# Sparse attention: the step pipeline begun behind the last query chunk, the last four projection chunks laid between and into its steps, one bank pair for the scores

## The chip, the cores and the metric

One of the cores of a Trainium2 chip runs the whole program; seven cores stand idle. The metric is the device time of one execution in microseconds (us). The engines are called TensorE (PE in the profile; PEld are its weight loads), VectorE (DVE), ScalarE (ACT), GpSimd (POOL) and SyncE (SP), which only issues transfers.

## The reference, cut to what matters

The program is two transformer stacks behind one another; the change touches the mixer of the second stack, which runs in each of its two layers (512 tokens, model width 1024). Cut to that mixer:

```
z = h @ w_in                      # q, kc, vc, ks, vs, kw, vw, gates, bg, cg, xc
# attention: 8 heads in 2 key groups, head width 64, queries in 4 blocks of 128
o_cmp = softmax(q . kc' , blocks already past) . vc'    # kc', vc': compressed blocks of 32 tokens, every 16
o_slc = softmax(rope(q) . rope(ks), causal) . vs        # 8 blocks of 64, of which up to 16 are chosen: all
o_win = softmax(rope(q) . rope(kw), causal, 512) . vw
attn  = g0 * o_cmp + g1 * o_slc + g2 * o_win            # g = sigmoid(gates)
# convolution group
conv  = bg * causal_conv3(cg * xc)
out   = concat(rms_norm(attn), rms_norm(conv)) @ w_out
```

## The kernel before, in words

All dense products run in split precision: weights and activations are each held as a rounded part and a remainder, and a product takes three matmuls (lo x hi, hi x lo, hi x hi). Weights come in **chunks** of 256 output columns (1 MB each). A ring of four buffers holds them: SP loads a chunk when the one four places before is finished (L2352), ACT rounds it (`split_next`, L637 to 645), POOL subtracts to get the remainder in four instructions (L2384), and TensorE does 48 matmuls of 128x512 with it (`chunk_products`, L413). ACT's list of splits is written out by hand and stands two chunks ahead of TensorE. DVE takes each result out of PSUM (`take`, L2085), which frees its bank pair. PSUM has four bank pairs: `main0` and `main1` for chunks in turn (`group_slot`, L463), `misc0` and `misc1` for everything else.

The mixer (`nsa_tensor` L1690, `nsa_scalar` L1931, `nsa_vector` L2084) has 16 projection chunks. Chunk 12 holds the second half of the queries, chunks 13 and 14 the second halves of cg and xc, chunks 15 and 16 bg. Chunks 17 to 20 are the output projection. Before the change the order on TensorE is: chunk 12, gates' transposes, chunk 13, the rotation of the second query half (`turn_q(1)`), the compressed scores, chunk 14, transposes of the compressed probabilities, chunk 15, chunk 16 with the scores of steps 0 and 1 in it, and then the rest of the **step pipeline**.

There are 24 steps (`STEPS`, L1655 to 1663). Steps 0 to 7 are query block 3 (512 keys), 8 to 15 block 2 (384 keys); each has one head pair m and one branch (selected or window). Steps 16 to 19 are block 1 (256 keys) and 20 to 23 block 0 (128 keys), each with both branches. Step s goes through the engines like this:

- TensorE `scores(s)` (L1757 to 1772) into a bank pair that alternates (`score_view`, L1678: misc1 for step 0, then main0 and main1). It waits until the maxima of step s-2 have been read.
- DVE adds the mask and takes the row maxima (L2277), one instruction per head and branch.
- ACT does the exponential with the row sum (L2055).
- DVE `shares` (L2240 to 2252): reciprocal of the sums, times the gates, scaling of the probabilities.
- TensorE `turn` (L1774 to 1783): transposes; ACT copies them to SBUF (L2047); TensorE `values` (L1785 to 1796) adds their products with the values in misc1 (bank m[3] for blocks 3 and 1, m[2] for 2 and 0). At a block's start `compressed_values` (L1821) opens the bank; at its end ACT copies it out and squares it (L2037, L2040), and DVE sums the squares (`group_sums`, L2259).

In iteration s of each engine's loop TensorE does scores s, turn s-2, values s-3; DVE the maxima of s, then the shares of s-1.

The **convolution group** shares these engines. DVE: `conv` (L2153 to 2161) and `gated` (L2171) for each half; ACT: squares (L2061); DVE: two sums (L2284, L2285); TensorE: `half_sums` (L1833, the sums over the partitions, recorded at L490); ACT: the square root (L2065), which needs another activation table than the exponential; DVE: reciprocal (L2290); TensorE: `half_spread` (L1837, recorded at L505); DVE: two multiplications (L2295); ACT: four rounded copies to `hid_hi` (L2071); DVE: four remainders (L2302). Before the change, counted in steps: squares in 3, sums in 4, half_sums in 5, root in 6, reciprocal in 7, half_spread in 8, multiplications in 9 and 10, copies in 11 to 14, remainders in 12 to 15.

Behind the steps TensorE goes on with the output projection (recorded at L1901), which begins with the convolution half of its rows.

## Time and profile before

| what | value |
|---|---|
| median of 3 runs | 3218.84 us (3215.92 to 3219.0) |
| profiled execution | 3219.82 us |
| its span, first to last instruction | 3217.7 us |
| mean granted TensorE clock | 0.997 |
| TensorE busy | 3171.8 us (99%) |
| VectorE / ScalarE / GpSimd busy | 1168.1 (36%) / 1185.8 (37%) / 1463.5 us (45%) |
| one weight split on ScalarE (L642) | 1910 ns, 275 of them |
| one remainder on GpSimd (L2384) | 1350 ns, four to a chunk |
| one chunk's load (1 MB) | 4.8 us from issue to landing |
| steps, scores 2 to output projection | layer 0: 1693.34 to 1765.89, layer 1: 2714.78 to 2788.98 |

A busy share is the time in which an engine has at least one instruction under way. Matmuls overlap one another, so a row's duration is longer than the distance to the next; where a price per matmul is wanted, the distance between two starts is read. Idle time of an engine that nobody waits for costs nothing.

### The profile page before, as it was taken

To read this page: it belongs to the slowest core of one execution; us is meant where nothing else is said; L and a number is where in the kernel's file an instruction comes from. 1 tells how busy PE (TensorE), PEld (TensorE's weight loads), DVE (VectorE), ACT (ScalarE), POOL (GpSimd) and SP (SyncE) were. 2 spreads that over 40 slices of the span, in tenths; PEclk is the share of its full clock that TensorE was granted. 3 is DMA by queue.
4 is the path that set the end of the run, shared out by engine and by line. 5 is a ranking of instruction groups with operands and counts; after the bars stand their busy time and mean duration, and the time that the engine had idled before them with its cause. 6 is when DMAs were issued, how large, how long until landed. Compare 5 with 4: busy or idle time off the path is not lost.

```text
span 3217.7 us, 39225 instructions
## 1 busy us (share of the span) xinstructions
PE 3171.8 (99%) x15716; PEld 2602.9 (81%) x15716; DVE 1168.1 (36%) x1727; ACT 1185.8 (37%) x1432; POOL 1463.5 (45%) x1116
## 2 busy tenths in 40 slices
PE   9999999999999999999999999999999999999998
PEld 7888888888888888888776888888888877788887
DVE  6534331343434112211858522104221376742212
ACT  4544332434443233322428423224322243742322
POOL 4335544433554554444650454454444382154443
PEclk9999999999999999999999999999999999999999
DMA  4113223212222222222420222222222241022222
GB/s 163 66 54 117 91 96 113 97 66 90 94 91 104 99 98 104 91 105 105 141 82 15 79 96 99 98 100 90 104 91 105 83 163 69 21 86 101 95 102 94
DMA packets 47672, 302.53 MB, mean 94 GB/s; under 512 B 5680, under 2 KB 8752, under 8 KB 12352
## 3 DMA queue, kind: packets, MB, share of 16 engines
q1 hardware_dynamic: 42480, 292.85, 25.5%
q10 hardware_dynamic: 5072, 7.90, 0.8%
q8 instruction: 97, 1.59, 0.2%
q14 instruction: 23, 0.19, 0.0%
HBM read 296.54 MB, written 2.10 MB: 93 GB/s over the span
## 4 chain that ended last, share of the span: by engine, by line
issue 46%; POOL 35%; PE 16%; ACT 1%; DVE 1%; DMA 0%; POOLq 0%; SPq 0%; ACTq 0%; DVEq 0%
POOL w_lo L2384 35%; PE main L430 13%; PE main L1901 1%; PE main L572 1%; ACT b_p L2055 0%; DMA stage<-in_w 0%; DVE b_p L2277 0%; ACT b_pT L2047 0%; PE misc L490 0%; DVE b_p L2252 0%; DVE y L892 0%; POOLq L98 0%; POOLq L2382 0%; PE main L1770 0%; PE misc L1792 0%
## 5 line engine op out<-in xcount | busy, mean ns | idle before, releaser
L2384 POOL TENSOR_TENSOR w_lo<-stage,w_hi 128x512 fp32r<-128x512 f32 x1100 | 1448.7, 1350 | 1722.7 <-ACT w_hi L642 1722.7
L430 PE MATMUL main<-h_hi,w_lo 128*128 128x512 f32 x2456 | 961.4, 391 | 1.1 <-POOL w_lo L2384 0.7
L430 PE MATMUL main<-h_lo,w_hi 128*128 128x512 f32 x2456 | 956.6, 390 | 0.0
L430 PE MATMUL main<-h_hi,w_hi 128*128 128x512 f32 x2456 | 956.5, 389 | 0.0
L642 ACT ACTIVATE w_hi<-stage 128x2048 fp32r<-128x2048 f32 x275 | 523.0, 1910 | 418.1 <-DMA stage<-in_w 417.0
L430 PEld LDWEIGHTS main<-h_hi,w_lo 128*128 128x128 f32 x2456 | 461.7, 188 | 103.0 <-issue 7.2
L430 PEld LDWEIGHTS main<-h_hi,w_hi 128*128 128x128 f32 x2456 | 461.5, 188 | 96.6
L430 PEld LDWEIGHTS main<-h_lo,w_hi 128*128 128x128 f32 x2456 | 461.7, 188 | 94.9 <-issue 0.5
L430 PE MATMUL main<-hid_hi,w_lo 128*128 128x512 f32 x1168 | 454.5, 389 | 0.0
L430 PE MATMUL main<-hid_hi,w_hi 128*128 128x512 f32 x1168 | 454.4, 389 | 0.0
L430 PE MATMUL main<-hid_lo,w_hi 128*128 128x512 f32 x1168 | 454.4, 389 | 0.0
L430 PEld LDWEIGHTS main<-hid_hi,w_lo 128*128 128x128 f32 x1168 | 219.2, 188 | 45.7 <-issue 0.2
L430 PEld LDWEIGHTS main<-hid_hi,w_hi 128*128 128x128 f32 x1168 | 219.2, 188 | 45.6
L430 PEld LDWEIGHTS main<-hid_lo,w_hi 128*128 128x128 f32 x1168 | 219.2, 188 | 45.4
L826 DVE TENSOR_TENSOR val<-main,rstd 128x1024 f32<-128x1024 f32 x60 | 73.5, 1224 | 461.1 <-PE main L430 461.1
L695 ACT ACTIVATE hid_hi<-val 128x1024 f32 (+1 forms) x66 | 69.9, 1059 | 371.2 <-DVE val L832 371.2
L806 DVE TENSOR_TENSOR gate<-main,rstd 128x1024 f32<-128x1024 f32 x66 | 80.8, 1224 | 328.3 <-PE main L430 299.2
L859 DVE TENSOR_SCALAR y<-main,par 128x512 f32<-128x512 f32 x48 | 36.0, 750 | 378.3 <-PE main L430 330.3
L836 DVE TENSOR_TENSOR hid_lo<-val,hid_hi 128x1024 f32 (+1 forms) x66 | 89.4, 1355 | 93.0 <-ACT hid_hi L695 93.0
L690 ACT ACTIVATE sq<-gate 128x1024 f32<-128x1024 f32 x44 | 46.7, 1061 | 184.6 <-DVE gate L824 184.1
L851 DVE TENSOR_TENSOR x<-main,x 128x1024 f32<-128x1024 f32 x16 | 19.6, 1225 | 246.0 <-PE main L430 246.0
L832 DVE TENSOR_TENSOR val<-val,sq 128x1024 f32<-128x1024 f32 x66 | 86.3, 1307 | 7.8
(342 smaller groups left out, 3145.2 us busy)
## 6 DMA issues: line engine op xcount, KB each, us to landing
stage<-in_w SPq DMA_DIRECT2D x275, 1024.0 KB, 4.8
x<-in_xT SPq DMA_DIRECT2D x8, 256.0 KB, 5.1
out_x<-x ACTq DMA_DIRECT2D x4, 512.0 KB, 2.6
stage<-in_w SPq DMA_DIRECT2D x8, 128.0 KB, 6.1
stage<-in_w SPq DMA_DIRECT2D x2, 512.0 KB, 7.4
b_r<-sq ACTq DMA_DIRECT2D x4, 256.0 KB, 7.1
b_r<-sq ACTq DMA_DIRECT2D x4, 255.5 KB, 8.6
ev_ws<-in_ev_ws ACTq DMA_DIRECT2D x1, 512.0 KB, 6.0
```

The costliest lines, as they stand in the source:

```text
L430: last = pe.matmul(acc[:, m, :], w[a], r[b], start=start and k == 0 and j == 0, stop=stop and k == nk - 1 and j == 2)
L572: last = pe.matmul(acc[:, m, :], w[a], r[b], start=start and k == 0 and j == 0, stop=k == nk - 1 and j == 2)
L642: act.activation(c.w_hi[:, s, :, :].rearrange("p k n -> p (k n)"), c.stage[:, s, :], ACT.Copy)\
L690: e.activation(c.sq[:, :, :], c.gate[:, :, 2:], ACT.Silu).then_inc(c.act_ready, 1)
L695: e.activation(two(c.hid_hi, i), c.val[:, :, :], ACT.Copy).then_inc(c.hid_hi_done, 1)
L806: e.tensor_tensor(c.gate[:, :, 2:], c.ps[n.slot()][:, :, :], rstd, ALU.mult)\
L826: e.tensor_tensor(c.val[:, :, :], (c.mp[1] if extra else c.ps[n.slot()])[:, :, :], rstd, ALU.mult)\
L832: e.tensor_tensor(c.val[:, :, :], c.val[:, :, :], c.sq[:, :, :], ALU.mult)\
L836: e.tensor_tensor(two(c.hid_lo, i), c.val[:, :, :], two(c.hid_hi, i).bitcast(F32), ALU.subtract).then_inc(c.hid_lo_done, 1)
L859: return dve.tensor_scalar(c.y[:, 2 * m + b, :], acc[:, b, :], c.par[:, col:col + 1], None, ALU.mult)
L1901: last = pe.matmul(acc[:, m, :], w[a], r[b], start=start and k == k0 and j == 0, stop=stop and k == k0 + 3 and j == 2)
L2384: last = e.tensor_tensor(c.w_lo[:, s, k:k + 2, :].rearrange("p k n -> p (k n)"), c.stage[:, s, k * CW:(k + 2) * CW], c.w_hi[:, s, k:k + 2, ...
```

## The change

- TensorE: the gates' transposes move into chunk 12 (before its sixth k tile). Chunk 13 is done in three pieces by the new function `chunk_tiles`: k tiles 0 and 1; then the query rotation, the compressed scores and scores 0; k tiles 2 to 4; scores 1; k tiles 5 to 7. Chunks 14, 15 and 16 are done in three pieces each inside steps 2 to 10 (`FILL`), between turn and values, all in the same bank pair (`same_slot`). The compressed probabilities' transposes stand in step 2, before turn 0.
- All scores go to one bank pair, the other one than the chunks'. Scores s waits for the maxima of step s-1, and scores 0 for the rotated queries.
- The convolution group: the takes stand in steps 2, 5, 8 and 11, the second half's convolution in steps 5 and 6, the gatings in 8 and 11. The rest of its chain is counted from `CONV_STEP` = 11: squares in 12, sums in 13, half_sums in 14, root in 15, reciprocal in 16, half_spread in 17, both multiplications in 18, copies in 20 to 23, remainders in 21 to 24. Its sums use bank m[3] instead of m[2], so that `compressed_values(1)` (step 19) waits for the multiplications instead of `compressed_values(2)` (step 11). Its squares go to other tiles.
- ACT: the mask's transfer is issued behind the rotated queries, two weight splits stand in steps 4 and 8, the copies of the compressed probabilities in step 2.
- DVE: the product with the cosine stands before the wait for the rotation; the normalizing of the compressed probabilities stands behind the maxima of step 0.

```diff
+def chunk_tiles(pe, n, c, acc, k0, k1):
+    s = n.chunk % RING
+    if k0 == 0:
+        pe.wait_ge(c.w_lo_done, n(c.w_lo_done))
+    for k in range(k0, k1):
+        for m in range(2):
...
+            for j, (a, b) in enumerate(((1, 0), (0, 1), (0, 0))):
+                last = pe.matmul(acc[:, m, :], w[a], r[b], start=k == 0 and j == 0, stop=k == KT - 1 and j == 2)
+    if k1 == KT:
+        last.then_inc(c.chunk_done, 1)
+        n.chunk += 1
+def same_slot(pe, n, c):
+    pe.wait_ge(c.group_taken, n.group)
+    n.skip(c.group_taken)
+    n.group += 1
+    n.flip += 1
+    return c.ps[n.slot(-1)]
+FILL = {2 + 3 * j + q: r for j in range(3) for q, r in enumerate(((0, 3), (3, 6), (6, KT)))}
+CONV_STEP = 11
 def score_view(c, l, s):
-    return c.mp[1] if s == 0 else c.ps[(s - 1 + c.score_slot[l]) % 2]
+    return c.ps[c.score_slot[l]]
@@ scores
-        if s < 3:
-            pe.wait_ge(c.group_taken, n.group - (s < 2))
+        if s == 0:
+            pe.wait_ge(c.q_roped, 2 * l + 2)
         else:
-            pe.wait_ge(c.a_max, 64 * l + exps_until(s - 1))
+            pe.wait_ge(c.a_max, 64 * l + exps_until(s))
@@ compressed_values, half_sums
-        if i == 2:
+        if i == 1:
             pe.wait_ge(c.half_done, n(c.half_done, 2))
-        pe.wait_ge(c.a_sum, 5 * l + 1)
-        token_sums(pe, c.m[2], c.ones, c.acc[:, 0, :], True, True).then_inc(c.half_ssq, 1)
+        pe.wait_ge(c.a_sum, 5 * l + 2)
+        pe.wait_ge(c.a_oT, 4 * l + 1)
+        token_sums(pe, c.m[3], c.ones, c.acc[:, 0, :], True, True).then_inc(c.half_ssq, 1)
@@ TensorE's order
-    z()
-    rope_was_read()
-    gates_turn()
-    z()
+    z(at={5: lambda: (rope_was_read(), gates_turn())})
+    acc = group_slot(pe, n, c)
+    c.score_slot[l] = n.slot()
+    chunk_tiles(pe, n, c, acc, 0, 2)
     pe.wait_ge(c.a_gate_exp, l + 1)
     turn_q(1)
     pe.wait_ge(c.tok_copied, n(c.tok_copied))
     compressed_scores()
-    z()
-    rope_was_read()
-    compressed_prob_turn()
-    z()
-    c.score_slot[l] = n.slot(1)
-    z(at={4: lambda: scores(0), 6: lambda: scores(1)})
+    scores(0)
+    chunk_tiles(pe, n, c, acc, 2, 5)
+    scores(1)
+    chunk_tiles(pe, n, c, acc, 5, KT)
     for s in range(2, N_STEPS + 3):
         if s < N_STEPS:
             scores(s)
-        if s == 5:
+        if s == 2:
+            rope_was_read()
+            compressed_prob_turn()
+        if s == CONV_STEP + 3:
             half_sums()
-        if s == 8:
+        if s == CONV_STEP + 6:
             half_spread()
         if 2 <= s < N_STEPS + 2:
             turn(s - 2)
+        if s in FILL:
+            if FILL[s][0] == 0:
+                acc = same_slot(pe, n, c)
+            chunk_tiles(pe, n, c, acc, *FILL[s])
@@ ACT's steps
+        if s == 2:
+            for hh in range(2):
+                act.wait_ge(c.a_probT, 50 * l + hh + 1)
+                act.activation(c.b_pcT[:, hh, :], c.m[hh][:, :], ACT.Copy).then_inc(c.a_copied, 1)
-        if s == 3:
+        if s in (4, 8):
+            split_next(act, n, c)
+        if s == CONV_STEP + 1:
             act.wait_ge(c.conv_done, n(c.conv_done))
...
-        if s == 6:
+        if s == CONV_STEP + 4:
             act.wait_ge(c.half_ssq, n(c.half_ssq))
...
-        if 11 <= s < 15:
+        if CONV_STEP + 9 <= s < CONV_STEP + 13:
@@ DVE's steps
         if s == 2:
-            take(c.val[:, :, :])
-            gated(1)
-            signal(c.conv_done)
+            take(c.b_u[1][:, :, :])
+        if s in (5, 8, CONV_STEP):
+            take_again(c.val[:, :, :])
...
+        if s == 0:
+            compressed_shares()
         if 1 <= s <= N_STEPS:
             shares(s - 1)
-        if s == 4:
+        if s == 5:
+            conv_input(1)
+            conv_taps(2)
+        if s == 6:
+            conv_taps(3)
+        if s == 8:
+            gated(0)
+        if s == CONV_STEP:
+            gated(1)
+            signal(c.conv_done)
+        if s == CONV_STEP + 2:
...
-        if s == 7:
+        if s == CONV_STEP + 5:
...
-        if 9 <= s < 11:
-            if s == 9:
-                dve.wait_ge(c.half_spread, n(c.half_spread))
-            x = c.b_y[:, 2 * s - 18:2 * s - 16, :]
-            dve.tensor_tensor(x, x, over_tiles(c.m[2][:, :]), ALU.mult).then_inc(c.half_done, 1)
+        if s == CONV_STEP + 7:
+            dve.wait_ge(c.half_spread, n(c.half_spread))
+            for j in range(2):
+                x = c.b_y[:, 2 * j:2 * j + 2, :]
+                dve.tensor_tensor(x, x, over_tiles(c.m[3][:, :]), ALU.mult).then_inc(c.half_done, 1)
-        if 12 <= s < 16:
+        if CONV_STEP + 10 <= s < CONV_STEP + 14:
```

## Rows read from the trace of the kernel before

**Rows 1.** Waits of TensorE in the steps of layer 0: total, times, longest (us).
```profile
PE misc L1781 <- DVE b_p L2252: 2.4, 4, 1.1
```
**Rows 2.** Stretches of layer 0: length, busy us per engine, clock, DMA share, GB/s.
```profile
1693.30:1723.60 30.30, 28.46 (x262) 19.23 (x262) 24.10 (x76) 25.04 (x56) 0.00 (x0) 1.00 0.08 34
...
1723.60:1765.90 42.30, 39.54 (x417) 28.61 (x415) 37.52 (x167) 39.68 (x130) 0.00 (x0) 1.00 0.01 2
...
1742.80:1765.20 22.40, 21.16 (x243) 16.26 (x241) 19.56 (x106) 22.35 (x80) 0.00 (x0) 1.00 0.01 2
```
**Rows 3.** Timeline of TensorE where scores 0 interrupts chunk 16: start, duration, what.
```profile
1683.59 0.39 PE L430 MATMUL main<-h_hi,w_hi 128*128 128x512 f32 x1
1683.91 1.13 PE L1770 MATMUL misc<-b_k,b_qr 64*128 64x512 f32 x4
1684.97 0.50 PE L430 MATMUL main<-h_hi,w_lo 128*128 128x512 f32 x1
1685.31 0.39 PE L430 MATMUL main<-h_lo,w_hi 128*128 128x512 f32 x1
1685.54 0.40 PE L430 MATMUL main<-h_hi,w_hi 128*128 128x512 f32 x1
```
**Rows 4.** Timeline of TensorE in the steps of layer 0; idle time in brackets.
```profile
1693.34 1.13 PE L1770 MATMUL main<-b_k,b_qr 64*128 64x512 f32 x4 [1.31 <-DVE val L2087]
...
1705.37 1.05 PE L490 MATMUL misc<-ones,acc 128*128 128x1 f32 x8 [1.36 <-DVE acc L2285]
1706.29 1.07 PE L1781 MATMUL misc<-ident,b_p 128*128 128x128 f32 x8
...
1708.31 1.13 PE L1770 MATMUL main<-b_k,b_qr 64*128 64x512 f32 x4
...
1711.42 1.13 PE L1770 MATMUL main<-b_k,b_qr 64*128 64x512 f32 x4
...
1715.38 0.65 PE L505 MATMUL misc<-ident,col 128*128 128x128 f32 x4
...
1729.74 0.92 PE L1770 MATMUL main<-b_k,b_qr 64*128 64x384 f32 x4
...
1732.20 0.92 PE L1770 MATMUL main<-b_k,b_qr 64*128 64x384 f32 x4
```
**Rows 5.** Timeline of ACT in the steps of layer 0.
```profile
1700.88 1.05 ACT L2061 ACTIVATE val<-b_y 128x1024 f32<-128x1024 f32 x1
...
1712.57 1.28 ACT L2065 ACT_TABLE_LOAD   x1
1713.87 0.26 ACT L2065 ACTIVATE col<-misc,stat 128x4 f32<-128x4 f32 x1
...
1715.12 1.28 ACT L2055 ACT_TABLE_LOAD   x1
...
1736.46 0.71 ACT L2071 ACTIVATE hid_hi<-b_y,par 128x512 fp32r<-128x512 f32 x1
```
**Rows 6.** Timeline of DVE in layer 0: a product beside GpSimd and without, sums, scaling.
```profile
1626.36 2.20 DVE L2155 TENSOR_TENSOR b_u<-b_u,val 128x1024 f32<-128x1024 f32 x1
...
1668.05 1.23 DVE L2155 TENSOR_TENSOR b_u<-b_u,val 128x1024 f32<-128x1024 f32 x1
...
1703.37 1.22 DVE L2284 TENSOR_TENSOR sq<-sq,val 128x1024 f32<-128x1024 f32 x1
1704.63 0.69 DVE L2285 TENSOR_TENSOR acc<-sq 128x512 f32<-128x512 f32 x1
...
1721.19 1.22 DVE L2295 TENSOR_TENSOR b_y<-b_y,misc 128x1024 f32<-128x1024 f32 x1
```
**Rows 7.** Layer 1 behind the wait for the sums: a stretch, then TensorE's timeline.
```profile
2728.00:2730.00 2.00, 2.00 (x20) 1.83 (x20) 1.10 (x4) 1.60 (x4) 0.00 (x0) 0.69 0.00 0
...
2728.73 1.97 PE L1792 MATMUL misc<-b_pT,b_va 128*64 128x128 f32 x16
2730.63 1.89 PE L1770 MATMUL main<-b_k,b_qr 64*128 64x512 f32 x4
```

More of the change, by code:

```diff
@@ L2020, in nsa_scalar @@
     split_next(act, n, c)
+    act.wait_ge(c.q_roped, 2 * l + 2)
+    act.dma_start(c.b_amask[:, :], a["b_amask"]).then_inc(c.b_masks_loaded, 16)
     act.wait_ge(c.a_cmp_sub, l + 1)
-    act.dma_start(c.b_amask[:, :], a["b_amask"]).then_inc(c.b_masks_loaded, 16)
     act.activation(c.b_p[:, 2, :, :], c.b_p[:, 2, :, :], ACT.Exp).then_inc(c.a_cmp_exp, 1)
-    split_next(act, n, c)
-    for hh in range(2):
-        act.wait_ge(c.a_probT, 50 * l + hh + 1)
-        act.activation(c.b_pcT[:, hh, :], c.m[hh][:, :], ACT.Copy).then_inc(c.a_copied, 1)
-    split_next(act, n, c)
     groups = 0
@@ L2151, in flat, with conv_input, conv_taps @@
             n.skip(c.a_lo_done)
[L2153 removed]
+    def conv_input(j):
         u = c.b_u[j]
         step(dve.tensor_tensor(u[:, :, :], u[:, :, :], c.val[:, :, :], ALU.mult))
[L2156 to L2161 removed]
+    def conv_taps(m):
+        u = c.b_u[m // 2]
+        w = [c.par[:, PC["cw"] + 12 * l + 4 * k + m:][:, 0:1] for k in range(3)]
+        step(dve.tensor_scalar(c.b_y[:, m, :], u[:, m % 2, :], w[2], None, ALU.mult))
+        for k, s in ((1, 1), (0, 2)):
+            step(dve.scalar_tensor_tensor(c.b_y[:, m, s:], u[:, m % 2, 0:T - s], w[k],
+                                          c.b_y[:, m, s:], ALU.mult, ALU.add))
     def hidden(kv):
@@ L2209, in nsa_vector @@
     rope_k(1)
-    conv(0)
+    conv_input(0)
+    conv_taps(0)
+    conv_taps(1)
     take(c.b_q[:, 2:4, :], HD ** -0.5)
@@ L2227, in nsa_vector, with compressed_shares, take_again @@
         .then_inc(c.a_cmp_sub, 1)
-    dve.wait_ge(c.a_cmp_exp, l + 1)
-    step(dve.tensor_reduce(cst, prob, AX.X, ALU.add))
-    step(dve.reciprocal(cst, cst))
-    rows = c.b_cst[:, :, :].rearrange("p h (i m) -> p h i m", i=TT)
-    step(dve.tensor_tensor(rows, rows, c.b_g[:, :, 0:8].rearrange("p i (h m) -> p h i m", h=2), ALU.mult))
-    dve.tensor_tensor(prob, prob, cst.unsqueeze(2).to_broadcast([P, 32, 32]), ALU.mult)\
-        .then_inc(c.a_cmp_norm, 1)
-    take(c.val[:, :, :])
-    conv(1)
-    take(c.val[:, :, :])
-    gated(0)
+    def compressed_shares():
+        dve.wait_ge(c.a_cmp_exp, l + 1)
+        step(dve.tensor_reduce(cst, prob, AX.X, ALU.add))
+        step(dve.reciprocal(cst, cst))
+        rows = c.b_cst[:, :, :].rearrange("p h (i m) -> p h i m", i=TT)
+        step(dve.tensor_tensor(rows, rows, c.b_g[:, :, 0:8].rearrange("p i (h m) -> p h i m", h=2), ALU.mult))
+        dve.tensor_tensor(prob, prob, cst.unsqueeze(2).to_broadcast([P, 32, 32]), ALU.mult)\
+            .then_inc(c.a_cmp_norm, 1)
+    def take_again(dst):
+        n.flip += 1
+        take(dst)
     def shares(s):
```

41 lines of the change are left out of this document (18 added, 23 removed).

## Prediction

> **What bounds the kernel now.** TensorE is nearly always busy over the whole run, and the change touches only the sparse-attention stage, which runs once in each of two layers. So only TensorE time inside that stage can be won. I read three views of it: the waits, the stretches and the timelines. The stage has two kinds of TensorE work: projection chunks (48 matmuls, one every 0.23 us [rows 3]) and 24 attention steps. In a step TensorE does scores, eight transposes ("turn") and value products; DVE takes the row maxima and scales the probabilities; ACT does the exponentials and copies the turned probabilities out of PSUM.
>
> In the waits of layer 0, TensorE stands still for DVE's scaled probabilities four times, 2.4 us together [rows 1]. The timeline adds 1.31 us before scores 2 and 1.36 us before the conv group's sum of squares [rows 4]. Those are the holes that chunk work could fill, some 5 us and in the other layer the same.
>
> The stretches show what lies beneath. From scores 2 to scores 11 (30.3 us) ACT is busy for 25.0 and DVE for 24.1, so both have room. From scores 11 to the output projection (42.3 us) ACT is busy 39.7, DVE 37.5, TensorE 39.5. In the last 22.4 us of that, ACT is busy for 22.35: there ACT, not TensorE, sets the pace [rows 2]. I call the first stretch the front and the second the tail. The question is what each gets.
>
> **The front.** The three chunks that stood ahead of the steps now lie in steps 2 to 10, nine pieces of 12 to 18 matmuls, 2.7 to 4.1 us each, and a fourth is split around scores 0 and 1. A full-width step of 3.1 us (scores 7 behind scores 6 [rows 4]) becomes one of 6 to 7.4 us, against some 2.5 us of ACT and DVE work in a step. So the waits in the front go: 1.4 (scores 2) + 0.3 (the first of the four) + 1.4 (the sum of squares) = 3.1 us. The conv group's sums and spread leave the front too: 0.9 us (the sums start at 1705.37, the next group 0.92 later) and 0.5 us for the spread [rows 4]. They come back in the tail.
>
> What is added: each extra change between chunk matmuls and other ones costs 0.09 us going out (0.32 instead of 0.23) and 0.11 coming back (0.34 instead of 0.23) [rows 3]. There were five such pairs, there will be twelve: 7 x 0.2 = 1.4 us. The compressed probabilities' transposes now stand directly before turn 0, which must wait until ACT has emptied the same banks: a copy of half a microsecond against half a microsecond of transposes, 0.3 us. Front: -3.1 - 1.4 + 1.7 = **-2.8 us**.
>
> Edits that I cost at nothing, each with its cover. Scores 0 now waits for the rotated queries: TensorE has 12 chunk matmuls, the rotation and the 64 small matmuls of the compressed scores to do while DVE takes, rotates and adds; by my walk the cover is about 1 us, and what DVE is later than that is paid whole. The score mask's DMA is issued on ACT's queue only then and has to land before the first maximum; DVE's maximum and subtraction for the compressed scores cover it, and the 18 chunk matmuls behind scores 0 cover both for TensorE. Two weight splits (1.9 us of ACT each) move from before the steps to steps 4 and 8, where ACT has 4 us to spare; GpSimd's four subtractions behind each of them come later, but their chunks are used only after the steps. SP's loads hang on finished chunks and come later by the same time. One bank pair for scores means that scores s+1 waits for the maxima of step s instead of s-1. In the front a 6 us step covers that. In the tail TensorE has turn and values (1.6 us for 384 keys, 2.0 for 512) against maxima of 1.0 to 1.4 us: covered while DVE is on time, a wait when it is late.
>
> **The tail.** Here comes the bill. The conv group's tail (second gating, squares, sums, square root, spread, scaling, splitting) moves from steps 2 to 15 to steps 11 to 24, so these land in a stretch where ACT and DVE are full:
> - ACT: the two squares, 1.9 us, and the square root with its table load and the exponential's reload, 2 x 1.28 + 0.3 = 2.8 us [rows 5]. The four copies to hid_hi, 0.6 us each start to start, were in steps 11 to 14; they now fall in steps 20 to 23, inside the 22.4 us in which ACT has no gap.
> - DVE: a take and a gating (2.4 us), the sums (1.22 + 0.69) and the scaling, of which one piece of 1.22 was still in the front [rows 6]: 5.5 us.
> ACT's work in the tail becomes 39.7 + 1.9 + 2.8 = 44.4 us, DVE's 37.5 + 5.5 = 43.0 us, both more than the 42.3 us that the tail takes now. That alone is the lower bound: with no idle time at all, 44.4 us, +2.1. The upper bound is the same work with the idle time ACT has now (42.3 - 39.7 = 2.6) and the new waits on top. Of these there are two. The sum of squares: a step is 2.46 us here (1729.74 to 1732.20) instead of 3.11, so its chain of ACT squares and DVE sums has 0.65 us less cover: a wait of about 2.0 instead of 1.36 us [rows 4]. And group 1's first products in step 19 now wait for the conv scaling that DVE does in one piece of 2.3 us in step 18, behind maxima and scaling: about 1.5 us for TensorE, but ACT is busy all the same by then. Taking 44.4 + 2.6 + 1.0 (the waits, as far as ACT starves for them) = **48.0 us**, +5.7 us, is near the upper bound. I take it because walking the three engines' lists step by step leaves ACT idle for some 4 us in steps 12 to 15, where the copy of turn 12 hangs on the sum of squares, and without a gap afterwards.
>
> On table loads the rows show 1.28 us each, with the next activation 0.02 us behind the first [rows 5]. The Trainium skill ("ScalarE: Activation LUTs", What ACT_TABLE_LOAD costs) gives the same 1283 ns and another 1380 ns of drain for every switch. By that page the two switches would be 5.3 us, and the sum 2 x 2.7 us higher; the rows leave no room for such a drain, and I go by them.
>
> Per layer -2.8 + 5.7 = +2.9 us, for both layers **+5.8 us**. The profiled execution took 3219.82 us, 2.1 more than its span of 3217.7, and is 1.0 above the median of the runs, 3218.84; I put the difference on the median: **3224.6 us**, +0.18%. Differences under 0.2% (6.4 us) are about what a measurement of this kernel can't tell from no change.
>
> **The rivals.**
> *A, ACT keeps up (chance 0.22).* The new waits hide in one another and ACT never starves: the tail is 44.4 us. -2.8 + 2.1 = -0.7 per layer, 3217.4 us. For it: ACT's work is packed to within 0.05 us over 22.4 us there already. Against: in the rest of the tail ACT stands for 2.6 us even now.
> *B, the full gain (0.13).* The tail stays at 42.3 us or sheds its own waits too, since more time between chunk and step lets ACT and DVE enter it early. -2.8 x 2 gives 3213.2, and with the clock's fall in layer 1 (below) gone 3211.6. Against it stands the sum of 44.4 us of ACT work.
> *C, the clock falls (0.18, slower).* The granted clock stands at 2.4 GHz nearly throughout. In layer 1, right behind the 1.36 us wait for the sums, it fell to 1.2 GHz (0.69, the mean of a stretch that holds both levels); a step's value products took 1.97 us and the next scores 1.89 where scores take 1.13 [rows 4, 7]; with 0.8 us lost on each, 1.65 us. In layer 0 the same wait cost no fall. With 2.0 us at the sums and 1.5 us in step 19 it may fall at both places in both layers: four falls for one, 3 x 1.65 = 5.0 us, 3229.6 us. It decides if TensorE's idle share at these places exceeds that of 1.36 us in a step. The Trainium skill ("TensorE: Matmul & The Clock Gate", What's actually happening) has it that the throttled rate is the default and activity releases it; the trace agrees, and by that rule the fills protect the front while the tail is more exposed.
> *D, a drain at the table loads (0.03, slower).* Were each load followed by a stop as long as itself, ACT would lose 2 x 1.28 us more per layer: 3229.7 us.
> *E, DVE against GpSimd (0.04, slower).* DVE's product of two SBUF tensors took 2.20 us beside GpSimd's subtractions and 1.23 us without [rows 6]. Step 5 has a take, maxima, shares, the conv input and three taps, 7 us, 10 so slowed, against 7.4 us of TensorE; one step of slack absorbs it. If it did not, 3 us per layer: 3230.6 us.
> That nothing is hidden at all (the chunks only displace, no wait goes) would be +3.1 per layer on top of the forecast and needs front waits that I see no cause for.
>
> **How the numbers follow.** The forecast has 0.40, its own range 3221 to 3228. Outside it, A and B reach down to 3212, C, D and E up to 3231; 3212.5 to 3231 leaves about 2 in 10 out. Faster by over 0.2% (below 3212.4) needs B with some more, and part of my doubt in the tail's walk: 0.14. Slower by over 0.2% (above 3225.3): C, D, E and somewhat under half of the forecast: 0.42. Within: 0.44.
>
> **What would show it.** In the changed kernel: scores 11 comes about 2.8 us earlier after chunk 12's start; steps 2 to 10 show no idle time on TensorE over 0.3 us; the wait for the sums of squares is near 2 us and stands in step 14; the first group-1 products wait for the conv scaling; ACT is busy over 97% from step 15 to the last value product, and scores 11 to output projection takes about 48 us. If that stretch is under 44 us, or TensorE's waits there sum to less than 5 us, the forecast's mechanism is wrong; if TensorE waits inside steps 2 to 10, the front is.

## The result, and the profile after

The changed kernel took **3235.99 us** (median of 5 runs, 3230.44 to 3238.7) against 3218.84 us before, ratio 1.0053 [1.0042, 1.0063]: 17 us slower, where +5.8 was forecast and 3231 was the top of the range. The profiled execution took 3234.93 us, its span is 3232.8 us.

Three views are needed, in this order. First TensorE's waits in the changed kernel (total, times, longest, us):

```profile
PE misc L1809 <- DVE b_p L2293: 6.2, 6, 1.4
...
PE misc L516 <- DVE acc L2339: 4.0, 2, 2.0
...
PE misc L1858 <- DVE b_y L2349: 3.1, 2, 1.5
PE misc L1820 <- ACT b_pT L2081: 1.7, 2, 0.9
```

The wait for the sums of squares is 2.0 us, the one for the scaling 1.5: both as forecast. Both layers are in these rows: scaled probabilities are now waited for 3.1 us in a layer, 2.4 before [rows 1]. Next the stretches of the changed kernel: chunk 12 to scores 11 (the front) and scores 11 to the output projection (the tail), first layer 0, then layer 1 (length; busy us of PE, PEld, DVE, ACT, POOL; clock; DMA share; GB/s):

```profile
1627.36:1723.14 95.78, 95.44 (x583) 69.81 (x581) 62.10 (x120) 36.17 (x72) 27.42 (x20) 0.96 0.16 56
1723.14:1774.20 51.06, 43.23 (x428) 31.50 (x426) 41.55 (x171) 43.68 (x131) 0.00 (x0) 0.95 0.07 22
...
2659.11:2751.79 92.68, 92.34 (x583) 68.07 (x582) 62.04 (x120) 36.17 (x72) 27.40 (x20) 1.00 0.16 58
2751.79:2803.76 51.97, 44.10 (x428) 32.02 (x426) 41.54 (x171) 43.68 (x131) 0.00 (x0) 0.93 0.06 21
```

The same cuts in the kernel before, beside the tail shown in [rows 2]:

```profile
1625.57:1723.63 98.06, 94.94 (x595) 71.56 (x594) 64.18 (x124) 39.95 (x74) 28.15 (x20) 0.98 0.18 65
...
2648.59:2746.70 98.11, 94.99 (x595) 71.29 (x592) 64.34 (x124) 39.95 (x74) 28.17 (x20) 0.98 0.18 65
2746.70:2788.98 42.28, 39.52 (x417) 28.59 (x415) 37.51 (x166) 39.66 (x130) 0.00 (x0) 1.00 0.01 2
```

The front became 2.3 and 5.4 us shorter, the tail 8.8 and 9.7 us longer. The two layers differ in the clock column, which stands at 1.00 in one front and at 0.96 in the other. The third view is therefore TensorE's timeline in step 14, in the changed kernel's layer 0:

```profile
1734.59 1.18 PE L516 MATMUL misc<-ones,acc 128*128 128x1 f32 x8 [2.00 <-DVE acc L2339]
1735.63 1.52 PE L1809 MATMUL misc<-ident,b_p 128*128 128x128 f32 x6
1737.08 1.55 PE L1820 MATMUL misc<-b_pT,b_va 128*64 128x128 f32 x12
```

and in layer 0 of a second profile of the same kernel (run e11 below), where the clock stayed up:

```profile
1728.98 1.05 PE L516 MATMUL misc<-ones,acc 128*128 128x1 f32 x8 [2.00 <-DVE acc L2339]
1729.89 0.85 PE L1809 MATMUL misc<-ident,b_p 128*128 128x128 f32 x6
1730.68 0.88 PE L1820 MATMUL misc<-b_pT,b_va 128*64 128x128 f32 x12
```

The same transposes take 1.52 us instead of 0.85 and the same value products 1.55 instead of 0.88: 1.2 GHz instead of 2.4 (a stretch of 3 us there, 1735 to 1738, has a granted clock of 0.56). Where no fall stands behind step 14, the changed kernel's stage looks like this (e11, layer 0; the fourth row is where the low clock does stand in that layer, from 1.1 us before the tail's end on):

```profile
1624.88:1717.52 92.64, 92.30 (x583) 68.08 (x582) 62.01 (x120) 36.19 (x72) 27.52 (x20) 1.00 0.17 58
1717.52:1767.04 49.52, 41.66 (x429) 30.26 (x427) 41.55 (x171) 43.60 (x131) 0.00 (x0) 0.99 0.06 23
...
1735.00:1765.90 30.90, 25.36 (x278) 19.23 (x276) 27.27 (x125) 30.39 (x97) 0.00 (x0) 1.00 0.01 1
1765.90:1769.40 3.50, 3.41 (x14) 2.60 (x15) 1.04 (x1) 1.13 (x3) 0.00 (x0) 0.51 0.00 0
```

Step 23 with what follows it takes 9.89 us in this layer and 9.43 in layer 1 of the first profile, where no fall stands at the tail's end. So a tail of 49.5 us holds 0.45 us of lower clock, and without any fall the changed kernel's tail is 49.07 us.

So the loss has two parts, and every run gives an estimate of them: its time multiplied by its mean granted clock is about what it would take at 2.4 GHz throughout, the rest counts as lost to the lower clock. (The clock is listed to three digits, 1.6 us on one run either way, so I use means.) Over the 72 runs of the kernel before in all comparisons that is 3209.3 us and 8.9 us lost; over 10 runs of the changed kernel 3215.5 and 19.7. By this estimate **+6.2 us are the order of the work and +10.8 us are the clock.**

The estimate counts too much as lost, in both kernels. In the kernel before the clock is low in the last 7.7 us, where TensorE has no matmul:

```profile
3210.00:3217.70 7.70, 0.00 (x0) 0.00 (x0) 4.43 (x4) 0.00 (x0) 0.00 (x0) 0.50 0.63 253
```

And in e6 below it was low between the two layers' stages:

```profile
2599.00:2606.00 7.00, 6.02 (x29) 6.05 (x30) 6.93 (x6) 1.38 (x1) 5.54 (x4) 0.51 0.14 57
```

Yet from layer 0's output projection to layer 1's chunk 12 e6 takes 882.60 us, and the kernel before, with half as much time at the low clock there, 882.69.

The stretches give a second estimate. Without a fall the front goes from 96.35 to 92.66 us and the tail from 42.27 to 49.07: +3.1 us a layer. And 1.0 us a layer lies outside front and tail. 20 us before chunk 12 TensorE waits for GpSimd's remainder of a chunk's weights, 0.37 us in the kernel before and 1.34 in the changed one. Before, layer 1 (TensorE, the subtraction that it waits for, DVE's product with the cosine):

```profile
2629.09 0.47 PE L430 MATMUL main<-h_hi,w_lo 128*128 128x512 f32 x1 [0.37 <-POOL w_lo L2384]
2627.69 1.25 POOL L2384 TENSOR_TENSOR w_lo<-stage,w_hi 128x512 fp32r<-128x512 f32 x1
2629.57 1.71 DVE L2125 TENSOR_TENSOR gate<-b_q,b_cos 128x1024 f32<-128x1024 f32 x1
```

and after:

```profile
2639.60 0.47 PE L431 MATMUL main<-h_hi,w_lo 128*128 128x512 f32 x1 [1.34 <-POOL w_lo L2438]
2637.20 2.25 POOL L2438 TENSOR_TENSOR w_lo<-stage,w_hi 128x512 fp32r<-128x512 f32 x1
2636.64 1.68 DVE L2158 TENSOR_TENSOR gate<-b_q,b_cos 128x1024 f32<-128x1024 f32 x1
```

The change moved this product ahead of DVE's wait for the rotation. It now runs beside the subtraction, which takes 2.25 us instead of 1.25, and TensorE waits for it. The wait is 1.33 to 1.37 us in 28 of the 30 layers of the kernels with this edit, the hybrid e9 among them, which takes back the moves of ACT's splits and of DVE's takes; it is 0.37 us at most in the kernel before, e1 and e6, which do not have it. And e12, whose layer 0 has no fall at its tail's end either, takes 883.54 us from there to layer 1's chunk 12, 0.9 more than the kernel before. No run takes this edit back alone. Together that is 4.1 us a layer: by the stretches some 8 of the 17 us are the order of the work and some 9 the clock.

### The profile page after: what moved, and what is told of

Same layout as the page of the kernel before. It is cut to its first block, busy times and chain, and to the rows that moved or that the text cites. A ratio compares the mean times of both kernels' runs of the same rounds, so it can differ in the third digit from the quotient of the medians.

```text
span 3232.8 us, 39223 instructions
## 1 busy us (share of the span) xinstructions
PE 3177.9 (98%) x15716; PEld 2603.7 (81%) x15716; DVE 1171.2 (36%) x1727; ACT 1185.8 (37%) x1432; POOL 1463.5 (45%) x1116
## 4 chain that ended last, share of the span: by engine, by line
issue 46%; POOL 35%; PE 16%; ACT 1%; DVE 1%; DMA 0%; POOLq 0%; SPq 0%; ACTq 0%; DVEq 0%
POOL w_lo L2438 35%; PE main L431 11%; PE main L447 1%; PE main L1935 1%; PE main L598 1%; PE main L1798 1%; DMA stage<-in_w 0%; PE misc L1809 0%; PE misc L1820 0%; ACT b_p L2089 0%; PE misc L516 0%; DVE b_p L2318 0%; DVE y L918 0%; POOLq L98 0%; POOLq L2436 0%
## 5 line engine op out<-in xcount | busy, mean ns | idle before, releaser
L431 PE MATMUL main<-h_hi,w_lo 128*128 128x512 f32 x2328 | 910.5, 391 | 3.5 <-POOL w_lo L2438 3.2
L431 PE MATMUL main<-h_lo,w_hi 128*128 128x512 f32 x2328 | 906.3, 389 | 0.0
L431 PE MATMUL main<-h_hi,w_hi 128*128 128x512 f32 x2328 | 906.2, 389 | 0.0
L431 PEld LDWEIGHTS main<-h_hi,w_lo 128*128 128x128 f32 x2328 | 437.3, 188 | 97.9 <-issue 7.0
L431 PEld LDWEIGHTS main<-h_hi,w_hi 128*128 128x128 f32 x2328 | 437.3, 188 | 90.9
L431 PEld LDWEIGHTS main<-h_lo,w_hi 128*128 128x128 f32 x2328 | 437.4, 188 | 90.1 <-issue 0.5
L845 DVE SCALAR_TENSOR_TENSOR sq<-gate,par,sq 128x512 f32<-128x512 f32 x88 | 72.3, 842 | 45.8 <-ACT sq L709 39.7
```

The lines of the kernel that those rows point to most:

```text
L431: last = pe.matmul(acc[:, m, :], w[a], r[b], start=start and k == 0 and j == 0, stop=stop and k == nk - 1 and j == 2)
L845: e.scalar_tensor_tensor(c.sq[:, j, :], c.gate[:, j, k:k + T], c.par[:, bass.ds(col + 2 * i + j, 1)], c.sq[:, j, :], ALU.mult, ALU.add).th ...
```

## The experiments

All ratios are to the kernel before on the same chip. "At full clock" is the product just named, "lost" the rest. Front and tail are us in one profiled layer; those with * hold a fall of the clock that lengthens them by over 1 us. The tails of 49.4 and 49.5 without a * and e7's 51.6 hold 0.45 us of a fall at their end.

| run | median us (runs) | ratio | at full clock / lost | front | tail |
|---|---|---|---|---|---|
| before | 3217.8 (72) | 1 | 3209.3 / 8.9 | 98.1* | 42.3 |
| e11, changed kernel again | 3233.39 (5) | 1.0057 [1.0043, 1.0071] | 3215.2 / 20.1 | 92.6 | 49.5 |
| e1, conv late alone | 3233.39 (4) | 1.005 [1.0033, 1.0067] | 3213.8 / 18.6 | 93.5 | 49.4 |
| e2, two pairs from step 12 | 3233.72 (4) | 1.0047 [1.003, 1.0063] | 3217.3 / 15.4 | 92.7 | 49.5 |
| e3, waits filled, too much | 3234.25 (4) | 1.005 [1.0033, 1.0067] | 3217.5 / 17.0 | 92.6 | 51.2 |
| e3b, waits filled, less | 3230.58 (5) | 1.0038 [1.0024, 1.0052] | 3217.2 / 12.9 | 92.7 | 49.5 |
| e4, conv three steps earlier | 3230.45 (5) | 1.0037 [1.0023, 1.0052] | 3215.6 / 14.2 | 94.1* | 50.6* |
| e5, dense fills, conv early | 3221.97 (11) | 1.0011 [1.0002, 1.002] | 3211.7 / 10.3 | 95.6* | 45.2 |
| e10, the same, two pairs | 3221.0 (10) | 1.0008 [0.9999, 1.0018] | 3210.7 / 10.3 | 95.6* | 45.1 |
| e6, before, sums a step later | 3215.47 (10) | 0.9993 [0.9983, 1.0002] | 3208.1 / 8.0 | 95.0 | 43.1 |
| e9, hybrid | 3214.78 (11) | 0.9991 [0.9982, 1.0] | 3206.0 / 9.4 | 95.3* | 43.0 |
| e7, ACT dose, steps 20 to 23 | 3235.8 (4) | 1.0054 [1.0038, 1.0069] | 3218.6 / 17.0 | 92.7 | 51.6 |
| e12, DVE dose, steps 20 to 23 | 3228.44 (5) | 1.0037 [1.0022, 1.0051] | 3215.8 / 13.6 | 92.7 | 49.1 |
| e13, ACT dose, steps 13, 14 | 3231.52 (4) | 1.0046 [1.003, 1.0063] | 3215.6 / 17.0 | 92.7 | 49.5 |
| e15, DVE dose, steps 12 to 14 | 3234.67 (4) | 1.0052 [1.0035, 1.0069] | 3214.4 / 20.2 | 92.7 | 52.4* |
| e8, no table loads | 3232.99 (4) | 1.0047 [1.0032, 1.0062] | 3212.0 / 20.2 | 92.7 | 49.4* |
| e14, changed, sums a step later | 3233.8 (4) | 1.0045 [1.0028, 1.0061] | 3216.4 / 17.8 | 92.7 | 49.4 |

### Which part of the change costs

**e1: the kernel before, with nothing but the conv group's tail moved.**

```
-  if s == 5: half_sums()            (squares 3, root 6, spread 8, scaling 9 and 10)
+  if s == 14: half_sums()           (squares 12, root 15, spread 17, scaling 18)
```

> The kernel before, with the convolution group's chain alone moved to where the change has it (squares in step 12 to remainders in 21 to 24, sums in bank m[3], group 1 waiting for the scaling); chunks, scores' banks and everything else as before. Theory T (the loss is the chain in the full tail): the stretch from scores 11 to the output projection grows from 42.3 us to 49 to 52 us in both layers, the front loses its 1.4 us wait and 1.4 us of work, total +10 to +14 us over before. Rival R (the loss comes from the single score bank pair, or from the fills): within 3 us of before.

3233.39 us, 15 over the kernel before where 10 to 14 were expected: nearly the whole loss without a single chunk moved. Its stretches and its waits:

```profile
1624.28:1717.79 93.51, 91.89 (x584) 69.09 (x582) 61.66 (x122) 35.55 (x69) 28.14 (x20) 1.00 0.19 68
1717.79:1767.15 49.36, 41.50 (x429) 30.28 (x427) 40.41 (x170) 44.17 (x135) 0.00 (x0) 0.99 0.01 1
```

```profile
PE misc L490 <- DVE acc L2289: 4.3, 2, 2.1
...
PE misc L1831 <- DVE b_y L2299: 3.1, 2, 1.5
PE main L1771 <- DVE val L2090: 2.6, 2, 1.3
```

The tail is the changed kernel's. The front lacks the sums, the spread and the 1.36 us wait; against it the nine pieces of chunks gain only 0.85 us more (93.51 to 92.66).

**e2: the changed kernel with both bank pairs for the scores from step 12.**

```
+  return c.ps[(c.score_slot[l] + max(s - 11, 0)) % 2]      # scores(s) waits for the maxima of s - 2
```

> The changed kernel, with the scores alternating between both bank pairs from step 12 on, so that scores s waits for the maxima of step s-2 again. Theory T: the single pair costs only the 0.2 us wait at scores 14, so the time stays within 2 us of the changed kernel (about 3235). Rival R (one bank pair ties TensorE to DVE's lateness in the tail): the tail shrinks by 3 us or more a layer, 3229 us or less.

The tail stays at 49.5 us. The single pair isn't the cause.

**e4: conv group three steps earlier, the fills as halves of chunks in steps 2 to 7.**

```
-  FILL: steps 2 to 10, CONV_STEP = 11
+  FILL: steps 2 to 7, CONV_STEP = 8
```

> The changed kernel with each chunk laid into two steps instead of three (24 matmuls a piece, steps 2 to 7) and the convolution's chain counted from step 8 instead of 11 (takes in 4, 6, 8; splits in 3 and 6). Theory T: squares, sums and root fall into steps 9 to 12, the copies to hid_hi into 17 to 20; from scores 11 on ACT has some 4 us less to do, the sum of the attention stage shrinks by 3 to 5 us a layer, total 3225 to 3229 us. Rival R (fills as such cost, or the bank pair): within 2 us of the changed kernel.

3230.45 us, above the 3225 to 3229 that I expected. Two waits went and two came (TensorE's waits in e4):

```profile
PE main L1798 <- DVE b_nmax L2318: 4.7, 4, 1.6
PE misc L516 <- ACT sq L2070: 4.6, 2, 2.3
```

The sums use bank m[3], and three steps earlier ACT has not emptied it yet.

### Is it TensorE's idle time, or the clock behind it?

**e3 and e3b: matmuls that nothing reads in front of the two waits.**

```
+  for _ in range(k): pe.matmul(<free pair>[:, 0, 0:P], c.ident, c.ones)    # e3: 15 and 11, e3b: 8 and 6
```

> The changed kernel, with 15 small matmuls without use ahead of the wait for the sums of squares (step 14) and 11 ahead of the wait for the scaling (step 19), so that TensorE is active in these waits. Theory C (the falls of the clock behind these waits cost time of their own): no half-rate stretch behind step 14, the tail 1.5 to 3 us shorter a layer, total 3 to 6 us under the changed kernel. Rival (ACT's list sets the tail, what TensorE loses to the clock is hidden in it): the falls go but the time moves by less than 1.5 us.

e3 missed its 3 to 6 us: steps 14 and 19 became 6.7 and 6.4 us long instead of 5.4 and 5.6, a tail of 51.2 us. So a smaller dose was run beside the unchanged kernel.

> The changed kernel with 8 matmuls of 128 columns whose result nothing reads before the wait for the sums of squares, and 6 before the one for the scaling (15 and 11 were too many: they made the two steps longer). TensorE's idle time at both places is then under 0.5 us, the steps as long as without them. If the clock's falls behind these waits are a cause of the loss, no fall stands in steps 14 to 20 and the time is 3 to 6 us under the changed kernel's in the same batch (3229 to 3233 us). Rival: as many windows of low clock turn up elsewhere, so that the time stays within 2 us of it.

> The changed kernel once more, unchanged, in the same batch, as the measure for the others: 3233 to 3238 us, tail 49.4 to 49.5 us wherever the clock does not fall in it.

e3b's tails, layers 0 and 1:

```profile
1719.38:1768.89 49.51, 44.97 (x457) 33.50 (x455) 41.55 (x171) 43.57 (x131) 0.00 (x0) 0.99 0.06 23
...
2746.54:2796.03 49.49, 44.98 (x456) 33.51 (x454) 41.53 (x171) 43.58 (x131) 0.00 (x0) 0.99 0.07 23
```

and e11's tail in layer 1 with what follows it, for the clock:

```profile
2744.60:2797.18 52.58, 45.46 (x429) 32.97 (x427) 41.53 (x171) 43.72 (x131) 0.00 (x0) 0.90 0.06 21
2797.18:2860.00 62.82, 61.90 (x287) 51.91 (x286) 29.83 (x41) 22.84 (x30) 21.85 (x16) 0.95 0.18 68
```

TensorE is busy 45.0 us instead of 41.7, its wait in step 14 is gone and the one in step 19 is 0.2 us, and the stretch is the same to 0.02 us: TensorE's idle time is an effect. But no fall stands behind step 14, where one cost e11's layer 1 3.0 us (scores 20 come 34.85 us after scores 11 there and 31.81 in layer 0). In the nine profiles with a wait of some 2 us for the sums in step 14 and no busy-work (the changed kernel's two, e1, e2, e7, e8, e12, e13, e15), a fall stands behind it in 12 of 18 layers; in e3 and e3b in none of 4. The mean time of the changed kernel's ten runs is 3235.3 us, that of e3b's five 3230.1, 5.2 less, as expected (the medians of e11 and e3b are only 2.8 apart). So the clock is a real part, and one that busy-work takes back only in part: both layers of e3b still have the fall at the tail's end.

### Which engine sets the tail?

**e7, e12, e13, e15: one extra copy of 128 x 512 per step that nothing waits for**, on ACT in steps 20 to 23 (e7) or 13 and 14 (e13), on DVE in steps 20 to 23 (e12) or 12 to 14 (e15).

```
+  act.activation(<unused tile>, c.b_y[:, m, :], ACT.Copy)        # e7, e13
+  dve.tensor_copy(<unused tile>, c.b_y[:, m, :])                 # e12, e15
```

> The changed kernel with one more ACT copy (128 x 512, from b_y into a tile that nothing reads, some 0.6 us) in each of steps 20 to 23, which nothing waits for. If ACT sets the pace from the conv scaling to the output projection, each is paid whole: scores 11 to output projection 2.2 to 2.6 us longer per layer, time 3239.5 to 3242 us. Rival, TensorE or DVE sets it and ACT has slack: nothing per layer, 3235 to 3237 us. In between, the copies are paid in part.

> The changed kernel with one more DVE copy (128 x 512, SBUF to SBUF, nothing reads it) in each of steps 20 to 23, behind which the next maxima stand. If ACT alone sets the pace there, a DVE copy hides: scores 11 to output projection within 0.5 us of 49.5 where the clock does not fall. If DVE sets it too, the dose is paid, 1.2 to 2.4 us per layer. My guess is the first, paid to under a half.

> The changed kernel with one more ACT copy (128 x 512) in each of steps 13 and 14, before the square root, that nothing waits for. By the prediction's walk ACT stands idle there for lack of turn 12's copy, so both hide: tail within 0.4 us of 49.5 where the clock does not fall. Rival: ACT is the bound from the squares on, and the tail grows by the two copies, 1.0 to 1.3 us.

> The changed kernel with one more DVE copy (128 x 512, 0.42 us by the dose in steps 20 to 23, into a tile that is written again before anything reads it) in each of steps 12, 13 and 14. If DVE sets the pace there, all three are paid, scores 11 to output projection is 1.0 to 1.3 us longer where the clock does not fall (50.5 to 50.8). Rival: TensorE's and ACT's own waits set it, the copies hide and the tail stays within 0.4 us of 49.5.

The tails of e7, e12 and e13:

```profile
2752.99:2804.56 51.57, 42.27 (x428) 30.89 (x426) 41.63 (x171) 45.64 (x135) 0.00 (x0) 0.97 0.07 22
```

```profile
2747.62:2796.69 49.07, 41.62 (x428) 29.95 (x426) 42.79 (x175) 43.63 (x131) 0.00 (x0) 1.00 0.06 23
```

```profile
1717.58:1767.09 49.51, 41.64 (x429) 30.26 (x427) 41.54 (x171) 44.51 (x133) 0.00 (x0) 0.99 0.07 23
```

ACT 2.04 us busier late: tail 2.05 us longer, paid whole, all of it behind scores 23, though the median didn't show it (at full clock +3.4 on e11, and 3 us less lost to the clock). DVE 1.24 us busier late: nothing. Its 49.07 us are 0.45 under e11's 49.52 because this layer has no fall at its end (clock column 1.00), which is just what the fall costs there. ACT 0.9 busier early: nothing. e15's layers both hold the fall at step 14. Against e11's layer 1, which holds it too, its layer 1 is 0.4 us longer (52.99), and TensorE reached the sums 0.3 us later: the one copy ahead of DVE's sums was paid, the two behind them were not, where 1.0 to 1.3 us were expected. So DVE sets the pace up to its sums in step 14, ACT from step 16 to the end.

**e8: no table loads.** The square root is replaced by a plain copy; the root of the conv group's mean square is left out of the computation.

```
-  act.activation(c.col[:, 0:4], c.m[3][:, 0:4], ACT.Sqrt, bias=c.eps, scale=1.0 / 512)
+  act.activation(c.col[:, 0:4], c.m[3][:, 0:4], ACT.Copy, scale=1.0 / 512)
```

> The changed kernel with the square root of the conv group's mean square replaced by a plain copy, so that the root is left out and ACT loads no other table in step 15 and none back in step 16: 2.5 us of ACT less in the tail. If ACT sets the tail's pace from there, scores 11 to output projection is 2.0 to 2.6 us shorter per layer, time 3230.5 to 3233 us. Rival: the loads lie where ACT waits anyway (behind the sums, ACT had idle time in steps 12 to 15), tail shorter by under 0.7 us, time within 1.5 us of the changed kernel. If the change were worth over 3 us a layer, a drain at the loads (rival D of the prediction) would be in it.

By the product 3.2 us less than e11, but with four and five runs that is rough, and both its layers hold a fall in steps 14 and 15. The steps behind the fall say it better: step 18 takes 2.89 us against 3.90 and step 19 5.43 against 5.60, the others from 16 on are the same. That is 1.2 us a layer for 2.4 us less of ACT (41.21 against 43.60): paid by half, where 2.0 to 2.6 were expected if ACT set the pace alone.

**e14: the changed kernel with its sums a step later** (`half_sums` in step 15, root 16, reciprocal 17, spread 18).

> The changed kernel with the sums of squares, the root, the reciprocal and the spread one step later each (15, 16, 17, 18); the scaling stays in step 18. If the tail's length is ACT's work plus the idle time that step 14 gives it, the wait of 2.0 us before the sums and ACT's idle time of 2.3 us behind it go, scores 11 to output projection is 1.5 to 2.3 us shorter (47.2 to 48.0 where the clock does not fall), the clock's fall behind step 14 is gone too, and the time is 3226 to 3230 us. Rival: the sums are late by DVE's work and the next hand-over (the scaling, which now waits for a later spread in the same step) takes the same time again: tail 49 us or more, time 3230 us or more.

The rival was right: tail 49.45. Step 14 fell from 5.42 to 3.87 us and step 17 from 3.18 to 2.70, and steps 15 and 19 gave it back (2.46 to 3.35, 5.60 to 6.78). ACT's idle time from scores 11 to step 16 was 4.2 us in e11 and is 4.1 us here, in other places (its timeline, idle time in brackets):

```profile
1722.49 0.87 ACT L2081 ACTIVATE b_pT<-misc 128x384 f32<-128x384 f32 x2 [1.27 <-PE misc L1809]
...
1729.64 0.61 ACT L2089 ACTIVATE b_p<-b_p,b_nmax 128x384 f32<-128x384 f32 x1 [0.49 <-DVE b_nmax L2318]
...
1732.46 0.87 ACT L2081 ACTIVATE b_pT<-misc 128x384 f32<-128x384 f32 x2 [1.51 <-PE misc L1809]
...
1735.14 0.87 ACT L2081 ACTIVATE b_pT<-misc 128x384 f32<-128x384 f32 x2 [0.62 <-PE misc L1809]
```

### Versions with the conv group early

**e6: the kernel before, its sums one step later.**

```
-  sums 5, root 6, reciprocal 7, spread 8
+  sums 6, root 7, reciprocal 8, spread 9
```

> The kernel before with only the sums of squares, the root, the reciprocal and the spread one step later each (6, 7, 8, 9), no chunk moved. My theory of the front is that TensorE's 1.36 us before the sums are a plain wait that one more step covers, and that the clock's fall in layer 1 hangs on it: front 1.3 to 1.4 us shorter per layer, tail 42.3 as before, time 3214 to 3217 us, the fall behind step 5 of layer 1 gone. Rival: ACT and DVE set the steps 3 to 10 too, the idle time turns up at the next probabilities instead: front unchanged within 0.4 us, time 3217 to 3220.

```profile
1626.77:1721.75 94.98, 93.29 (x596) 70.39 (x594) 63.41 (x121) 39.52 (x73) 28.15 (x20) 1.00 0.19 67
1721.75:1764.82 43.07, 39.58 (x417) 28.56 (x415) 38.26 (x172) 40.34 (x131) 0.00 (x0) 1.00 0.01 2
```

The wait for the sums is gone and the clock column is at 1.00: 3.1 us of front in the layer, 0.8 given back in the tail. Only 1.4 of the 3.1 us are the wait. The other 1.7 are layer 0's fall, which stood at 1654 to 1657 in the kernel before, 50 us ahead of this wait, so that its absence here is no work of this edit; layer 1's fall stood behind the wait, and is gone too. In time 2.8 us, at the edge of what these runs can tell: the interval still holds no change.

**e5 and e10: each chunk whole in steps 2, 3 and 4, conv group as early as that allows**, with one pair (e5) or with both from step 15 (e10).

```
+  FILL = {2: (0, KT), 3: (0, KT), 4: (0, KT)}; CONV_STEP = 5      # sums 9, root 10, spread 12, scaling 12 and 13
```

> The changed kernel with the same three chunks laid whole into steps 2, 3 and 4 (one a step, 11 us each) instead of in nine pieces, and the conv group's tail moved back to where it stood: second take in step 5, squares in 6, sums and root in 8 and 9, scaling in two pieces in steps 11 and 12. The sums and the spread are written into the free main bank pair. My theory is that the loss sits in the tail because the conv group's work lands where ACT and DVE are full: then scores 11 to output projection is back at 42 to 43 us, the front stays near 93 us, the waits before the sums and before group 1's first products are gone, and the time is 3209 to 3214 us, faster than both kernels. Rival 1, one bank pair (scores s+1 behind the maxima of s) costs in the tail by itself: tail 45 us or more. Rival 2, any rearrangement is paid back, since ACT then has no lead from the front: front near 96, time 3217 to 3222.

> The dense version (three chunks whole in steps 2 to 4, conv group early) with the scores alternating between both bank pairs from step 15 on. If the single pair is what keeps its tail at 45.2 us (TensorE waited there for maxima, 3.7 us together), the waits for maxima from step 15 on are gone and the tail is 1.5 to 2 us shorter, time 3217 to 3219 us. Rival: DVE is late by itself and each such wait becomes one for the scaled probabilities: tail within 0.5 us of 45.2, time 3220 to 3223.

3221.97 and 3221.0 us: 13 us of the changed kernel's 17 are gone, but e5 misses its 3209 to 3214 us, and both stay above the kernel before. (The sums, the root and the scaling stand a step later in it than the expectation says.) With the scaling at the start of the tail, scores 14 waited 1.7 us for DVE's maxima in both; the second pair turned later waits for maxima into waits for probabilities, as the rival had it.

**e9: a hybrid meant to beat both.** Two more chunks ahead of the steps, one around scores 0 and 1, one in step 2.

```
+  FILL = {2: (0, KT)}; CONV_STEP = 3       # squares 4, sums 7, root 8, spread 10, scaling 10 and 11; two pairs from 13
```

> A version meant to beat both kernels, from what the runs have shown so far: two more chunks stand before the steps again, one is split around scores 0 and 1, and one alone is laid into step 2. The conv group's tail stands one step later than in the kernel before and two steps behind its sum (squares 4, sums 7, root 8, spread 10, scaling in steps 10 and 11), written into the pair that no scores use; from step 13 on the scores alternate between both pairs. By my account the front loses the waits of 1.3 and 0.3 us around scores 2 and the 1.36 us before the sums (front near 93.8 us), the tail is as in the kernel before (42.3 to 43.1), time 3211 to 3215 us. Rival: the waits on DVE only move by a step, as in the dense version: front plus tail at 138 us or more, time 3216 to 3221.

3214.78 us, 0.9991 [0.9982, 1.0] of the kernel before and some 20 us under the changed one: the fastest here, though its lead over e6 is less than these runs can tell. Its front of 95.28 us holds a fall of the clock (0.98), without which it would be near the 93.8 expected; tail 43.0. At full clock it is 3.3 us under the kernel before.

## Why the prediction was wrong

**The direction was right, and so was one of the two places named for the clock; the clock's price was not.** By its own steps:

- *Front, -2.8.* Without a fall of the clock the front before is 96.35 us (e6's 94.98 and the 1.36 it lacks), after 92.66: -3.7. The waits went as said, 0.34 came for the compressed probabilities as said, no other wait stood in steps 2 to 10. The term that was mis-sized is the changes between chunk and other matmuls, 1.4 us. By the timeline of e11 a change costs 0.09 going out and 0.1 back, but the chunk matmul follows the turn after 0.85 us where values follow it after 1.0: net 0.04 a pair, 0.4 us in all.

```profile
1664.80 1.10 PE L1809 MATMUL misc<-ident,b_p 128*128 128x128 f32 x8
1665.65 0.48 PE L447 MATMUL main<-h_hi,w_lo 128*128 128x512 f32 x1
...
1669.94 1.09 PE L1858 MATMUL misc<-b_pcT,b_vbd 128*64 128x128 f32 x16
```

- *Tail, 42.3 to 48.0.* It is 49.5, of which 0.45 are the fall at its end. ACT's work was put at 44.4 and is 43.6; its idle time at 3.6 and is 5.9. The walk had found the 4 us in steps 12 to 15, but the sum added only 1.0 to the 2.6 of before, as if the two overlapped. ACT in e11:

```profile
1722.28 0.87 ACT L2081 ACTIVATE b_pT<-misc 128x384 f32<-128x384 f32 x2 [1.27 <-PE misc L1809]
...
1730.46 0.87 ACT L2081 ACTIVATE b_pT<-misc 128x384 f32<-128x384 f32 x2 [2.28 <-PE misc L1809]
...
1734.99 1.28 ACT L2101 ACT_TABLE_LOAD   x1
1736.28 0.26 ACT L2101 ACTIVATE col<-misc,stat 128x4 f32<-128x4 f32 x1
...
1737.33 1.28 ACT L2089 ACT_TABLE_LOAD   x1
...
1767.16 0.60 ACT L2067 ACTIVATE b_oT<-misc 128x512 f32<-128x512 f32 x1 [1.22 <-PE misc L1820]
```

From 1735.00 to 1765.90 ACT is busy 30.39 of 30.90 us: packed, as forecast. The mistake is to take for a bound one engine's work over the whole stretch where DVE sets the first part and ACT the rest. Net of front and tail without falls +3.1 a layer, 6.2 in all, where 5.8 were forecast. That it comes so close is partly luck: the front's error of -0.9 and the tail's of +1.1 cancel.

- *DVE's product with the cosine, costed nowhere.* It is an edit of the change, but not in the list of those put at nothing. Rival E had the same collision of a DVE product with GpSimd, 2.20 us against 1.23 [rows 6], and looked for it in step 5 alone. Here GpSimd is the one held up, TensorE waits for it, and it costs 1.0 us a layer.

- *The clock, forecast at zero, +10.8 by the product and some 9 by the stretches.* **This is the step that failed.** The working kept the clock's losses as they were and gave rival C, the clock behind the waits of steps 14 and 19, a chance of 0.18 and 5.0 us on the forecast's waits. The mechanism is C's, and step 14 is one of its two places: in e11 the same wait of 2.0 us has a fall behind it in layer 1 and none in layer 0, as its timeline and stretches show. Behind step 19's wait neither profile of the changed kernel has one. The second place is the tail's end: TensorE has idle spots of 0.8, 1.4 and 0.9 us behind scores 23, and the clock fell there in three of the four layers, with the output projection's matmuls to pay for it (e11's layer 0: 0.45 us in the tail; 0.95 is the clock of the stretch behind layer 1). That these spots bring that fall on is argued, not shown: layer 1 of the first profile has the same ones, and no fall. C's price of 1.65 us fits the short fall in layer 0 of the first profile (1735.4 to 1738.8, 1.55 us); the falls behind step 14 in layer 1 of both profiles lasted twice as long (in e11 2755.8 to 2762.7) and cost 2.9 and 3.0. The rule of the Trainium skill ("TensorE: Matmul & The Clock Gate", What's actually happening) that the low clock is the default and activity lifts it is borne out by e3 and e3b, whose busy-work kept the clock up behind step 14. I cited it and gave it too little. I had also not seen that the front before held a fall in layer 0 as well (its clock column says 0.98). That one is behind no wait: it starts 3.8 us after the start of the compressed scores, 64 small matmuls without idle time between them. So do the falls in 16 of the 36 fronts profiled, in the old and the new order (2.7 to 4.7 us after that start), the changed kernel's layer 0 with its 3.1 us among them. Against these the fills protect nothing.
- *Rival A* (ACT keeps up) fell with the 5.9 us of idle time, *B* (the full gain) with the tail. *D*, the drain: the root follows its load after 0.01 us in e11, and leaving both loads out gave 1.2 us a layer, less than the loads' own 2.56. The Trainium skill ("ScalarE: Activation LUTs", What ACT_TABLE_LOAD costs) has a further 1380 ns of drain for each switch; no run here shows it. *E*: steps 2 to 10 had no wait over 0.34 us, so DVE kept up there; its collision came elsewhere, as said.

**Of what the text named as tests:** scores 11 came 3.7 us earlier after chunk 12 (2.8 said, clock left out), steps 2 to 10 had one wait over 0.3 us (0.34, the compressed probabilities', which the sum had), the sums' wait was 2.0 in step 14, group 1's products waited for the scaling, ACT was busy 97% from step 15 to the last value product, the tail was 49.5 (48). Nearly all held, and the time was still wrong, since none of them was a test of the clock.

**What stays open.** Where each unprofiled run lost its time to the clock: the profiled runs show only their own falls, at different places from run to run. What the changed kernel takes with the cosine's product where it was. And why moving the sums in e14 gave nothing at all. That its tail equals the others' to 0.1 us suggests that the hand-overs of the conv group through TensorE, ACT and DVE have to be paid once wherever they stand among full steps, but no run isolates this.

## What to carry to other kernels

Filling TensorE's gaps with foreign matmuls is worth only the gaps. What decides is what has to move to make room: here a chain of eight hand-overs went from steps where DVE and ACT had room [rows 2] into steps where they had none, and one of the two large gaps, with layer 1's fall behind it, was gone from the trace by moving four instructions by one step (e6; the time's interval still holds no change). Bound a stretch by the sum over its parts of whichever engine is full in each, not by one engine's total. Where a change adds idle time of 1 to 2 us to TensorE at several places, price the clock behind each of them as its own term, from traces of several runs; here it was as large as everything else. And give every moved instruction a line in the working, also one that only changes places with a wait: here one nobody priced cost 1.0 us a layer.

## What was not expected of the hardware

The same instructions with the same wait had the lower clock behind them in one layer and not in the other, so that runs of one kernel spread over 9 us (3230.81 to 3239.72) and a dose of 2.05 us a layer didn't show in a median (e7). And a low clock is a loss only where TensorE's work is waited for. Of the 8 to 10 us counted as lost even in the best orderings here (e6 8.0, e9 9.4) some 3 to 4 lie behind TensorE's last matmul, as in the kernel before.
